# Gate/up turns with two sets of four row tiles in seven products instead of one

## What is computed

```python
def swiglu(x, wg, wu, wd):
    return (jax.nn.silu(x @ wg) * (x @ wu)) @ wd
```

## Time and profile before

| | |
|---|---|
| Median of 3 runs | 1685.19 us |
| The profiled execution's own time | 1684.97 us |
| Its span | 1683.2 us |
| PE busy | 99% |
| DVE, ACT, POOL busy | 77%, 63%, 4% |
| Mean busy share of the DMA engines in the turns | 0.7 |
| Granted TensorE clock | 0.999 |

### The profile page before, as it was taken

How to read it: one execution, slowest core, us unless ns; L and a number is a source line. 1 busy time by engine, 2 the same in 40 slices (tenths; PEclk the granted TensorE clock), 3 DMA queues, 4 the chain that set the end, 5 groups by cost and what they waited for, 6 DMA issues and landing times.

```text
span 1683.2 us, 21057 instructions
## 1 busy us (share of the span) xinstructions
PE 1672.8 (99%) x7600; PEld 1378.7 (82%) x7600; DVE 1301.3 (77%) x1480; ACT 1061.1 (63%) x1519; POOL 64.4 (4%) x90
## 2 busy tenths in 40 slices
PE   9999999999999999999999999999999999999998
PEld 8888888888888888888777888888888888888887
DVE  7677777777758888867676866777777776889887
ACT  6566666666666555546665556666666666665554
POOL 1100000000000000002011000000000000000000
PEclk9999999999999999999999999999999999999999
DMA  8567777777764665655434556777777776556454
GB/s 293 179 215 221 227 220 223 228 221 225 226 208 164 211 214 184 227 191 185 150 126 150 178 195 175 223 223 224 222 226 223 224 223 237 173 200 229 171 208 167
DMA packets 168375, 345.42 MB, mean 205 GB/s; under 512 B 6132, under 2 KB 6260, under 8 KB 168184
## 3 DMA queue, kind: packets, MB, share of 16 engines
q1 hardware_dynamic: 162832, 324.67, 55.6%
q0 software_dynamic: 5184, 18.88, 7.5%
q10 hardware_dynamic: 296, 1.06, 0.2%
HBM read 323.61 MB, written 2.10 MB: 194 GB/s over the span
## 4 chain that ended last, share of the span: by engine, by line
PE 95%; DVE 2%; ACT 1%; DMA 1%; SPq 0%; issue 0%; ACTq 0%
PE acc L1728 12%; PE acc L1730 12%; PE acc L1729 12%; PE acc L1596 7%; PE acc L1598 7%; PE acc L1597 7%; PE acc L1816 6%; PE acc L1814 6%; PE acc L1815 6%; PE acc L1690 3%; PE acc L1688 3%; PE acc L1689 3%; PE acc L1801 2%; PE acc L1800 2%; PE acc L1799 2%; ACT prob L835 1%
## 5 line engine op out<-in xcount | busy, mean ns | idle before, releaser
L1179 DVE TENSOR_TENSOR w_lo<-raw,w_hi 128x1024 fp32r<-128x1024 f32 x342 | 411.9, 1218 | 166.1 <-ACT w_hi L730 164.7
L730 ACT ACTIVATE w_hi<-raw 128x1024 fp32r<-128x1024 f32 x342 | 354.7, 1057 | 213.2 <-PE acc L1730 179.2
L784 ACT ACTIVATE w_hi<-raw 128x1024 fp32r<-128x1024 f32 x215 | 227.2, 1061 | 189.3 <-PE acc L1816 114.0
L1729 PE MATMUL acc<-w_lo,xT_hi 128*128 128x512 f32 x864 | 336.1, 389 | 0.0
L1730 PE MATMUL acc<-w_hi,xT_lo 128*128 128x512 f32 x864 | 336.1, 389 | 0.0
L1728 PE MATMUL acc<-w_hi,xT_hi 128*128 128x512 f32 x864 | 336.1, 389 | 0.0
L1356 DVE TENSOR_TENSOR w_lo<-raw,w_hi 128x1024 fp32r<-128x1024 f32 x215 | 260.3, 1222 | 61.2 <-ACT w_hi L784 56.3
L1814 PE MATMUL acc<-w_hi,hT_hi 128*128 128x512 f32 x488 | 190.0, 389 | 0.2 <-DVE w_lo L1356 0.2
L1816 PE MATMUL acc<-w_hi,hT_lo 128*128 128x512 f32 x488 | 189.8, 389 | 0.0
L1815 PE MATMUL acc<-w_lo,hT_hi 128*128 128x512 f32 x488 | 189.8, 389 | 0.0
L1730 PEld LDWEIGHTS acc<-w_hi,xT_lo 128*128 128x128 f32 x864 | 162.2, 188 | 33.7
(11 more groups left out here) (202 smaller groups left out, 2292.0 us busy)
## 6 DMA issues: line engine op xcount, KB each, us to landing
raw<-w_gate_in SPq DMA_DIRECT2D x88, 1024.0 KB, 6.6
raw<-w_up_in SPq DMA_DIRECT2D x88, 1024.0 KB, 6.9
raw<-w_down_in SPq DMA_DIRECT2D x88, 1024.0 KB, 5.0
raw<-raw POOLq DMA_DIRECT2D x36, 512.0 KB, 5.5
raw<-w_q_in SPq DMA_DIRECT2D x16, 1024.0 KB, 5.0
raw<-w_o_in SPq DMA_DIRECT2D x16, 1024.0 KB, 5.0
raw<-w_kv_in SPq DMA_DIRECT2D x4, 1024.0 KB, 5.4
raw<-pool_w_in SPq DMA_DIRECT2D x3, 1024.0 KB, 12.9
```

The source lines that it names most:

```text
L730: nc.scalar.activation(w_hi[:, n % RING, :], raw[:, slot, off:off + 2 * C], ACT.Copy).then_inc(hi_ready, 1)
L1179: nc.vector.tensor_tensor(w_lo[:, n % RING, :], src, w_hi[:, n % RING, :].bitcast(F32), ALU.subtract).then_inc(unit_ready, 1)
L1729: nc.tensor.matmul(dst, xT_hi[:, k, tok], w_lo[:, n % RING, cols], start=False, stop=False)
```

## The change

The turn gets a second set: row tiles 0 to 3 are set 0, row tiles 4 to 7 set 1, each in seven products of six matmuls. Eight plain units are left (row tiles 8 to 15 of gate and of up), so a turn has 22 units. T1, T2, T3, B11 of both sets accumulate in the same banks. Set 0 reads gate load 0 in slot 0 and up load 0 in a fifth raw slot (4), set 1 reads gate load 1 in slot 1 and up load 1 in slot 3. [...] DVE makes T1 and T3 of each set, POOL's queue issues T2 and T4 of each. There is a second buffer for the token sums, and act_sums runs twice a layer. The turns are written out on SP, ACT, DVE and PE. 22 x 9 units are padded to a multiple of four in the counts (SUM_STEPS). The silu of a turn moves behind the first unit of the next one; the quad_moves move from behind units 7 to 10 to behind units 12 (two), 13, 15 and 20 (four, then act_hi).

The core of the diff:

```diff
-SUM_UNITS = 19
+SUM_SETS = 2
...
-SUM_ORDER = ["B11", ("gate", 2), ("gate", 3), "B21", ("gate", 4), "T1", ("gate", 5), ("gate", 6), "T3", ("gate", 7), "T2",
-             ("up", 2), ("up", 3), "T4", "B22", ("up", 4), ("up", 5), ("up", 6), ("up", 7)]
+SUM_ORDER = [("B11", 0), ("B11", 1), ("T1", 0), ("gate", 5), ("gate", 4), ("T1", 1), ("B21", 0), ("B22", 1),
+             ("B21", 1), ("B22", 0), ("gate", 6), ("gate", 7), ("T2", 0), ("T2", 1), ("T3", 1), ("T4", 0), ("T3", 0),
+             ("T4", 1), ("up", 5), ("up", 4), ("up", 6), ("up", 7)]
...
+SLOT_G, SLOT_U = (0, 1), (4, 3)
+TURN_LOADS = [("gate", 0, 0), ("gate", 1, 1), ("up", 0, 4), ("gate", 2, 2), ("up", 1, 3),
+              ("gate", 3, 2), ("up", 2, 2), ("up", 3, 3)]
...
+READ_LAST = {one: max(n for n, u in enumerate(SUM_ORDER)
+                      if turn_load(u) == one or u[0] in ("T2", "T4") and one == ("up", u[1])) + 1 for one in SLOT}
+SLOT_LAST = [max(READ_LAST[one] for one in SLOT if SLOT[one] == slot) for slot in range(RING + 1)]
...
             def load_sum_turn(l, j):
 
                 before = sum_units(l, j)
...
+                for n, (m, i, slot) in enumerate(TURN_LOADS):
+                    earlier = [one for one in TURN_LOADS[:n] if one[2] == slot]
+                    if earlier:
+                        sp.wait_ge(unit_ready, before + READ_LAST[earlier[-1][:2]])
+                    elif j > 1:
+                        sp.wait_ge(unit_ready, before - SUM_UNITS + SLOT_LAST[slot])
...
                     sp.dma_start(raw[:, slot, :].rearrange("p (k n) -> p k n", k=4),
-                                 w[:, 4 * i:4 * i + 4, bass.ds(j * C, C)]).then_inc(raw_in[slot], 16)
+                                 w[:, 4 * i:4 * i + 4, j * C:(j + 1) * C]).then_inc(raw_in[slot], 16)
```

ACT's turn after (each unit's rounding, then what is put behind it):

```diff
+                for n, unit in enumerate(SUM_ORDER):
+                    ac.wait_ge(unit_used, before + n - RING + 1)
+                    form, s = unit
+                    slot, off = turn_half(form, s)
+                    if turn_load(unit) not in landed:
+                        landed.add(turn_load(unit))
+                        ac.wait_ge(raw_in[slot], 16 * sum_loads(l, j, *turn_load(unit)))
+                    if form == "T2":
+                        ac.wait_ge(t2_in[s], 16 * (c + 1))
+                    elif form == "T4":
+                        ac.wait_ge(t4_in[s], 16 * (c + 1))
+                    elif form in ("T1", "T3"):
+                        ac.wait_ge(t_sum, sum_done(l, j, unit))
+                    nc.scalar.activation(w_hi[:, (before + n) % RING, :], raw[:, slot, off:off + 2 * C],
+                                         ACT.Copy).then_inc(hi_ready, steps_of(j, n))
+                    if n == 0 and j > 1:
+                        sum_silu(l, j - 1)
+                    if n == 10:
...
+                        nc.scalar.activation(common[:, 0, :], acc[:, P1, :], ACT.Copy).then_inc(p1_copied, 1)
+                    for part in {12: (0, 1), 13: (2,), 15: (3,), 20: (4, 5, 6, 7)}.get(n, ()):
+                        quad_move(l, j - 1, part)
+                    if n == 20:
+                        act_hi(l, j - 1)
```

DVE's turn after, the work behind each w_lo:

```diff
                     if n == 0:
+                        weight_sum(l, j, "T1", 0)
+                    if n == 2 and j > 1:
                         common_up(l, j - 1)
+                    if n == 3:
+                        weight_sum(l, j, "T1", 1)
+                    if n == 6:
+                        if j > 1:
+                            common_out(l, j - 1)
...
+                    if n in (8, 9):
+                        quad_turn(l, j - 1, n - 8)
+                    if n == 12:
+                        weight_sum(l, j, "T3", 1)
+                    if n == 13:
+                        weight_sum(l, j, "T3", 0)
+                    if n == 15:
...
+                    if n == 19:
...
+                    if n == 20:
+                        act_lo(l, j - 1)
```

weight_sum of T1 waits for the set's up load (raw_in), that of T3 for the sum T1 of its set. Behind n == 15 stands the add of P1's copy, behind n == 19 the other four adds of the turn. POOL:

```diff
+                    for s in (0, 1):
+                        gp.wait_ge(unit_ready, before + AT["T1", s] + 1)
+                        gp.dma_start(half("T2", s), half("B22", s), accum_op=ALU.add).then_inc(t2_in[s], 16)
+                    for s in (0, 1):
+                        gp.wait_ge(unit_ready, before + AT["B21", s] + 1)
+                        gp.wait_ge(t2_in[s], 16 * (c + 1))
+                        gp.dma_start(half("T4", s), half("T2", s), accum_op=ALU.add).then_inc(t4_in[s], 16)
...
-    nc = bacc.Bacc("TRN2", target_bir_lowering=False, num_devices=1)
+    nc = bacc.Bacc("TRN2", target_bir_lowering=False, num_devices=1, dynamic_dma_scratch_size=1024)
```

More of the change, by code:

```diff
@@ L449, in sum_units, with sum_loads, steps_of, sum_done @@
         def sum_units(l, j):
[L450 to L454, removed]
+            return (LAP_GU[l] + 2).units(SUM_UNITS * (j - 1))
+        def sum_loads(l, j, m, i):
+            slot = SLOT[m, i]
+            before = (LAP_GU[l] + 2).loads(slot) if slot < RING else SUM_LOADS[slot] * SUM_TURNS * l
+            return before + SUM_LOADS[slot] * (j - 1) + NTH[m, i]
+        def steps_of(j, n):
+            return 1 if j < SUM_TURNS or n + 1 < SUM_UNITS else 1 + SUM_STEPS - SUM_UNITS * SUM_TURNS
+        T_SUMS = [("T1", 0), ("T1", 1), ("T3", 1), ("T3", 0)]
+        def sum_done(l, j, unit):
+            return len(T_SUMS) * (SUM_TURNS * l + j - 1) + T_SUMS.index(unit) + 1
         def out_after(l, b):
@@ L541, in _ @@
             load_gate_up(0, 0)
-            with sp.Fori(1, NFB - 1) as j:
+            for j in range(1, NFB - 1):
                 load_sum_turn(0, j)
@@ L704, in _, with sum_silu @@
             squares(0, 0, 0, hblk)
[L706 to L740, removed]
+            def sum_silu(l, j):
                 ac.wait_ge(gate_sum, SUM_TURNS * l + j)
@@ L749, in gate_up @@
                     k0, tiles, off = UNITS_D[i % UD]
-                    round_hi(lap, i, tiles, off, shift=1 if not first and i < SUM_UNITS % RING else 0)
+                    round_hi(lap, i, tiles, off)
+                    if not first and i == 0:
+                        sum_silu(l, j - 1)
                     if first and l == 0:
@@ L817, in _ @@
             gate_up(0, 0, True)
-            with ac.Fori(1, NFB - 1) as j:
+            for j in range(1, NFB - 1):
                 sum_turn(0, j)
@@ L1684, in sum_product @@
                     te.wait_ge(unit_ready, before + n + 1)
+                    w = (before + n) % RING
                     for kk in range(2):
                         cols = slice(kk * C, (kk + 1) * C)
-                        x_hi, x_lo = hi(kk), lo(kk)
-                        nc.tensor.matmul(dst, x_hi, w_hi[:, n % RING, cols], start=start and kk == 0, stop=False)
-                        nc.tensor.matmul(dst, x_hi, w_lo[:, n % RING, cols], start=False, stop=False)
-                        last = nc.tensor.matmul(dst, x_lo, w_hi[:, n % RING, cols], start=False, stop=stop and kk == 1)
@@ L1729, in sum_turn @@
-                                nc.tensor.matmul(dst, xT_hi[:, k, tok], w_lo[:, n % RING, cols], start=False, stop=False)
-                                last = nc.tensor.matmul(dst, xT_lo[:, k, tok], w_hi[:, n % RING, cols], start=False,
-                                                        stop=stop)
-                        last.then_inc(unit_used, 1)
+                                dst, start, stop = pair_bank(gate if form == "gate" else up, t), starts[t], stops[t]
+                                nc.tensor.matmul(dst, xT_hi[:, k, tok], w_hi[:, w, cols], start=start and kk == 0, stop=False)
@@ new lines, in sum_turn @@
+                                nc.tensor.matmul(dst, xT_hi[:, k, tok], w_lo[:, w, cols], start=False, stop=False)
+                                last = nc.tensor.matmul(dst, xT_lo[:, k, tok], w_hi[:, w, cols], start=False,
+                                                        stop=stop and kk == 1)
+                            continue
+                        if form in ("B11", "B21", "T4"):
+                            k = 4 * s + (0 if form == "B11" else 2) + kk
+                            tok = second_tok if form == "T4" else first_tok
+                            x_hi, x_lo = xT_hi[:, k, tok], xT_lo[:, k, tok]
+                        else:
+                            row = {"T1": 0, "T2": 1, "T3": 2, "B22": 3}[form]
+                            x_hi, x_lo = s_hi[s][:, row, kk, :], s_lo[s][:, row, kk, :]
@@ L1734, in gate_up @@
+                        dst = banks[form]
+                        nc.tensor.matmul(dst, x_hi, w_hi[:, w, cols], start=starts[0] and kk == 0, stop=False)
+                        nc.tensor.matmul(dst, x_hi, w_lo[:, w, cols], start=False, stop=False)
+                        last = nc.tensor.matmul(dst, x_lo, w_hi[:, w, cols], start=False, stop=stops[0] and kk == 1)
+                    last.then_inc(unit_used, steps_of(j, n))
             def gate_up(l, j, first):
@@ L1821, in _ @@
             gate_up(0, 0, True)
-            with te.Fori(1, NFB - 1) as j:
```

(1 more changed line is left out.)

246 lines of the change are left out of this document (124 added, 122 removed).

## The result

The changed kernel takes 1726.42 us (median of four runs, 1725.15 to 1728.59) against 1685.01 us: 1.0248 times as long, 95% interval 1.0230 to 1.0266, 41.4 us more. The forecast was 1708 with a range of 1684 to 1745. PE does wait, at the place that was named; the clock falls in that wait as well.

The account below looks back on a forecast made before the run. PE, busy 99%, was taken as the bound: matmul count times pitch. 108 fewer matmuls give -24.5 us, new PE waits +47.7, so 1684.97 + 23.2 = 1708 us, range 1684 to 1745.

Parts of the forecast that it names:

- the place that was named: PE's wait for w_lo of product 21, the last unit of every turn: 2.4 us.
- Matmuls, -24.5 us: PE's turns: 180 matmuls instead of 186, 108 fewer in all at 0.2267 us each, if PE never waits.
- The path ahead of product 21: Each turn's end: late last up load, then quad_moves and act_hi on ACT, delay w_lo; PE waits 2.4 us.
- the second place: Start of each turn: queued loads bring up 0 late, stalling product 3; 0.25 us a turn, bounds 0 and 1.5.
- The sum of the waits: PE's waits at product 21 and at the turn's start: 2.4 + 0.25 us over 18 turns, +47.7 us.
- the clock: Rival: PE at half rate for 2 us after each new wait; +18 us, 1726 at least; chance 0.03.
- The accumulating DMAs: Rival: T2 and T4 transfers sharing one queue reach ACT 2 us late; +36 us, 1744; chance 0.14.
- Written-out loops: Turns as straight code on four queues cost nothing, since the down stage is written out already.
- second set of token sums: Second act_sums, first block: some 5 us more DVE work fits and costs nothing; uncovered, up to 5 us a layer.

Follow-up runs that it names:

- the kernel with slot 3 early: The changed kernel, but slot 3 is given back once unit 14, its real last reader, is rounded off, not unit 17: 1661.24 us.
- the quad_moves moved: The changed kernel, but its four last quad_moves stand behind unit 19 instead of unit 20: 1708.73 us.
- three small products: The changed kernel, but PE does three unused identity matmuls ahead of its wait for unit 21: 1723.14 us.
- slot 3 one unit earlier: The changed kernel, but the last up load waits for unit 16 instead of unit 17: 1697.08 us.
- six products: The changed kernel, but PE does six unused identity matmuls ahead of its wait for unit 21: 1718.74 us.
- half the quad_moves moved: The changed kernel, but two of its four last quad_moves stand behind unit 19, two still behind unit 20: 1707.00 us.

## Why the prediction came out as it did

- **Matmuls, -24.5 us: right.** With the waits gone, turns are 40.80 us and the kernel 23.5 us below the one before.
- **The path ahead of product 21: right, almost to the tenth.** It was to start with w_lo of 17 ending 2.86 us after product 14's start and to cost 2.4 us. PE was due at 264.92 (264.69 + 0.23), product 14 therefore at 251.3; w_lo of 17 ended near 254.2, 2.9 later, and 2.58 us were lost. The load took 5.2 where 5.1 was taken, and not because "nothing else is in flight there": three loads leave right behind it, as the prediction itself says under the second place. Its "that slot's last reader is T4" is wrong as well: T4 is the last unit that the code counts for slot 3, and the last that reads it is T3 of set 1. That the trace's loads take 5.1 us holds for the one at 198.2; their median was 6.9. Two experiments take the chain at either end, and the wait at product 21 goes.
- **The second place: right as a mechanism, but the 0.25 us a turn is met by luck.** In the change PE waits once in 18 turns ahead of product 3, 0.36 us, and never ahead of product 1. What a turn at full clock loses beyond the 2.58 us, 0.29 us, is mostly the slower matmuls behind the wait. The place shows its size only when product 21 no longer hides it: 45.8 us of DVE's waiting.
- **The sum of the waits**, 2.65 us a turn, measured 2.87 (43.67 less 40.80). So 18 x 0.22 = 4 us of the 18 us between forecast and result are here.
- **The term that failed is the clock**, a rival with 0.03 and nothing in the sum. "Less idle than that, which speaks against" compared the share of idle time, 2.65 of 43.5 us against 1.5 of 10. The share was the wrong measure; one wait of 2.6 us in a row did it, nine times of 18, and the longest wait that the trace before could show was 1.5 us. The price was 1 us a turn and is 1.5 us in every second one: 13.5 us, nearly all of the rest. No row of the kernel before shows the half rate or the 2 us in that rival's sum; in the trace of the change the granted clock is 0.50 for about 3.4 us at a time, in the turn shown from 0.4 us before the wait's end. That its 1726 us is the measured time is luck: 4.5 us too much for the clock stands against 4 too little for the waits. It was written as another case than the forecast's, too, where it is a consequence of the same wait and belongs in its sum.
- **The accumulating DMAs: refuted.** ACT never waits for one. Their share of the engines is 11.5% for twice the number, less than twice, and the engines reach 0.80 of a turn.
- **Written-out loops, second set of token sums at nothing: right within 1 us**; the first by its own run (1685.52 us), the second by the turns (40.80 us) and the total (1661.24) of the kernel with slot 3 early.

## What to carry to other kernels

Fewer instructions on the bounding engine pay only if each step's supply chain still fits: follow, for every load, the unit that gives its buffer back, the landing, and all that the rounding engine has queued behind it, and compare with the products that lie between. Give a buffer back at its real last reader; here one conservative term in a max over readers turned a gain of 24 us into a loss of 41. When a new long wait of TensorE is predicted, put the lower clock behind it into the same sum: here a granted clock of 0.50 came with some of the waits of about 2 us and more, at 1.5 us a turn in the change, and with none of 1.8 us or less.

## What the hardware showed unexpectedly

The granted clock fell behind single waits in turns that were otherwise busy throughout. By kernel, the longest wait in PE's list and the turns at half clock: 2.6 us in the change, nine of 18; 2.3 with the quad_moves moved, four; 2.0 with three small products, five; 1.8 with slot 3 one unit earlier, none; 1.3 with six products or with half the quad_moves moved, none. Which of two like waits is followed by a slow stretch, nothing in these rows tells.

A wait costs PE more than its list says. The list counts from the end of the last matmul, 0.39 us after its start, where the next would have started after 0.23: 2.42 us in the list are 2.58 lost. A matmul behind a wait is followed after 0.31 to 0.34 us at full clock instead of 0.23 (0.59 to 0.60 in seven of the change's 18), and those after it come at 0.23 to 0.24. So two short waits in a turn cost more than their sum: with half the quad_moves moved, 32.3 us in the list are 43.6 in the first two columns below. Added up on PE's timelines over the 18 turns, in us against a pitch of 0.227:

| Kernel | Gaps over 0.7 us (how many) | The matmul behind them | The rest: short gaps, slower matmuls, half clock | Sum | Reckoned |
|---|---|---|---|---|---|
| The change | 47.5 (18) | 3.8 | 13.9 | 65.2 | 47.7 |
| Quad_moves moved | 36.3 (28) | 2.7 | 7.6 | 46.6 | 30.6 |
| Half of them moved | 39.2 (44) | 4.4 | 2.7 | 46.3 | 30.6 |
| Slot 3 one unit earlier | 29.1 (19) | 2.1 | 5.0 | 36.2 | 24.3 |

The kernel with slot 3 early loses nothing by this count; its 1661.24 us and each sum give the four measured times within 1 us. So the 12 to 18 us by which the last three missed their expectations are found: the waits are 5 to 9 us longer in all than reckoned, and behind them come slower matmuls and, with the quad_moves moved, four stretches at half clock, for which the expectations had nothing.
